# Decode step of a hybrid NSA and latent-attention layer: compressed values from probabilities applied to cached tokens, and cache pages laid eight (latents four) tokens to a partition

## Chip, cores and metric

The kernel is one launch on one core of a Trainium2 chip. All data are fp32. The metric is the device time of the launch in microseconds. The engines named here are TensorE (PE), VectorE (DVE), ScalarE (ACT), GpSimd (POOL) and SyncE (SP); SP issues every DMA of the part of the kernel that is changed.

## What is computed

One decoder layer is applied to a prompt of 1024 tokens and to a decode batch of 8 rows with 4 new tokens each; each row has 2048 cached tokens in 16 pages of 128. Per decode row the reference computes, for the group of 8 NSA heads (2 key-value groups):

```
kc, vc = compress(k_cmp), compress(v_cmp)   # block n: sum over l < 32 of token[16 n + l] @ w[l], plus a constant
p_c    = masked_softmax(q . kc + bias)      # 127 blocks
o_cmp  = p_c @ vc
imp    = p_c @ overlap;  keep the 16 best of 33 blocks of 64 tokens (3 are forced)
o_sel  = softmax over the kept blocks of (q . k_sel + bias) @ v_sel
o_win  = softmax over the last 512 tokens @ v_win
o_a    = gate0 * o_cmp + gate1 * o_sel + gate2 * o_win
```

and for the 4 latent (MLA) heads `o_lat = softmax(q_lat . c + q_rope . k_rope) @ c` over all cached tokens. Then come an output projection and a last RMSNorm. A cached token has 512 numbers in the NSA cache (k_cmp, v_cmp, k_sel, v_sel, each 2 groups of 64) and 192 in the latent cache.

## The kernel before, in words

The launch first does the prompt (projection, preparation, attention, output tiles in `pe_out`), up to about 880 us. Then `pe_decode_loop` and its partners `dve_decode`, `act_decode`, `pool_decode` and `sp_decode` run over the 8 decode rows b = 0 to 7. A row is a fixed sequence written out by hand for each engine; the engines meet by semaphores, and nothing reorders them.

**Loads.** For each row SP reads 16 page numbers (`page_numbers`, L2470), loads 16 pages of the NSA cache (`load_pages`, L2478), the window and the keyed queries (L2489, L2387), and 16 pages of the latent cache (`load_latent`, L2483), then stores the window (L2495). Page n lies in `NSA[b % 2][:, n, :]`, one token to a partition, 2 KB each; latents likewise, 768 bytes each. There are two buffers: the pages of row b + 2 may be issued when `selected_values(b)` has ended (`s_avd`).

**TensorE, one row in order.** `key_products` (L2543) multiplies the turned keys by queries that already hold the key weights, into PSUM banks 3 and 4. `window_scores` (L2565). `compressed_scores` (L2574, L2578) gathers the products into scores on 32 partitions. `latent_scores` (L2592, and L2596 to L2598 for the new tokens) and between its parts `probabilities` (L2612 to L2614), which turns the compressed probabilities. `compress` (L2554): 32 products of 64 rows of turned value tokens by the value weights, for all 127 blocks; inside it the product `fmw` (L2623, which spreads minima over the partitions) and `importance` (L2619). Then `smw` (L2623, sums), `selected_scores` (L2605, into bank 5), `latent_values` (L2631), `window_values`, `compressed_values` (L2648), `fs` (L2623), `ss` (L2623), and at the end `selected_values` (L2653, L2655). In between stand the chunks of the next row (L2339): K0 to K3 turn its compressed keys, V0 to V3 its compressed values, four 128x128 transposes each. Each chunk is copied from PSUM by ACT or DVE into `XT` (L2725, L2730). In the last row a dummy product `keep_warm` (L489) stands ahead of `selected_values`.

**VectorE, one row in order.** Window minima; the compressed scores' minimum; after ACT's exponential the probabilities, also once multiplied by the gate; `selected_turn` (L2819), a transpose of the page keys for the selected scores of the same row; copy of the turned probabilities (L2861); reduction of the latent scores (L2864) and `spread` (L2801), which `fmw` on TensorE waits for; after `fmw` (L2867) the ranking of the blocks (L2871 to L2883); after `smw` scaling and `PTW`; the compressed values' constant (L2893); `PTM` (L2898), the turned latent probabilities that `latent_values` waits for; masking of the selected scores (L2901, L2904), their reduction (L2907) and `spread`, which `fs` waits for; after `ss` scaling and `PTS` (L2920), which `selected_values` waits for; then `window_turn` (L2812) and three `latent_turns` (L2796) of the next row.

**ScalarE.** Copy of the key products, exponentials (L2733), scale of the latent probabilities (L2747), copies of chunks (L2730).

**Order of small products.** Small results and chunks share three PSUM banks in a ring (`RING`); an entry may be written when the one three places earlier has been read.

Of the kernel before, what the change touches and what calls it, by code (L numbers as in the profile page):

```python
# [17 lines left out]
ALU = mybir.AluOpType  # L18
# [96 lines left out]
def build(nc, x_prompt, x_sample, cache_nsa, cache_mla, state_win, page_table, c_prompt, c_sample,  # L115
# [3 lines left out]
    with ExitStack() as ctx:  # L119
# [156 lines left out]
        s_ssq, s_ms, s_rstd, s_xn, s_xt = sem("s_ssq"), sem("s_ms"), sem("s_rstd"), sem("s_xn"), sem("s_xt")  # L276
# [594 lines left out]
        def act_squares(act, j):  # L871
# [3 lines left out]
            if j == 0:  # L875
                act.wait_ge(s_ms, 1)
# [218 lines left out]
        def dve_scale(dve, j):  # L1095

            n = rows(j)
            dve.wait_ge(s_rstd, j + 1)
            dve.tensor_scalar(xs(j)[0:n, :], xs(j)[0:n, :], RSTD[0:n, j:j + 1], None, ALU.mult)\
                .then_inc(s_xn, 1)  # L1100
# [30 lines left out]
        def pool_projection(pool):  # L1131
# [3 lines left out]
            pool.memset(SSQ[:, 0:1], 0.0).then_inc(s_ms, 1)  # L1135
# [58 lines left out]
        def pool_rstd(pool, j):  # L1194
# [4 lines left out]
                .then_inc(s_ms, 1)  # L1199
            pool.wait_ge(s_ms, j + 2)  # L1200
# [831 lines left out]
        def sp_out(sp, tiles, at):  # L2032
            for m, j in enumerate(tiles, at):
# [6 lines left out]
                if m == 2:  # L2040
                    load_queries(sp)
                    load_compressors(sp)
                    load_gates(sp)
# [18 lines left out]
        def pe_out(pe, tiles, at):  # L2062
# [14 lines left out]
            for m, j in enumerate(tiles, at):  # L2077
# [10 lines left out]
                for c in range(2):  # L2088
# [6 lines left out]
                    if m >= 5:  # L2095
                        chunk(pe, 0, ("K0", "K1", "K2", "K3", "V0", "V1")[2 * (m - 5) + c])
# [47 lines left out]
        def act_out(act, tiles, at):  # L2144
            copy = lambda o, i: act.activation(o, i, ACT.Copy)
            for m, j in enumerate(tiles, at):
# [7 lines left out]
                if m >= 5:  # L2154
                    read_chunk(act, copy, 0, ("K0", "K2", "V0")[m - 5])
# [11 lines left out]
        def dve_out(dve, tiles, at):  # L2167
            for m, j in enumerate(tiles, at):
# [25 lines left out]
                if m >= 5:  # L2194
                    read_chunk(dve, dve.tensor_copy, 0, ("K1", "K3", "V1")[m - 5])
# [19 lines left out]
        XT = view(20480, 4096).rearrange("p (k l n) -> p k l n", k=2, l=16)  # L2215
# [8 lines left out]
        VR = dsm(256).rearrange("p (s g e) -> p s g e", s=2, g=G)  # L2224
        PTI, PC, PG = dsm(192), dsm(132), dsm(132)
# [15 lines left out]
        WC2 = view(33152, 4096).rearrange("p (k l m) -> p k l m", k=2, l=16)  # L2241
        QWB = [view(33152 + 512 * n, 512).rearrange("p (l x) -> p l x", l=16) for n in range(2)]
        QSB = view(34176, 256).rearrange("p (b g q) -> p b g q", b=NB, g=G)
# [13 lines left out]
        FM, FI, DQ, HS, LOW = CE[:, 0:128], CE[0:RS, 128:256], CE[:, 256:260], CE[:, 260:262], CE[:, 262:712]  # L2257
# [3 lines left out]
        S_B, W_B, O_B = PS[:, 5, :], PS[:, 6, :], PS[:, 7, :]  # L2261
        W_WIN, W_NEW, W_MLA = W_B[:, 64:192], W_B[:, 192:256], W_B[:, 256:384]
# [5 lines left out]
        CHUNK_ITEMS = [f"K{c}" for c in range(4)], [f"V{c}" for c in range(4)]  # L2268
        SMALL_ITEMS = ["cmp", "pts", "fmw", "imp", "smw", "fs", "ss"]
        KEYED = {(m, c): str(m - 1) for m in range(1, 5) for c in range(2)}  # L2270
        RING = [(0, k + str(n)) for n in range(4) for k in "TAB"]
        RING += [(0, n) for n in CHUNK_ITEMS[0] + CHUNK_ITEMS[1]]
        FRONT = len(RING)
        for b in range(NB):
            more = (lambda *names: [(b + 1, n) for n in names]) if b + 1 < NB else (lambda *names: [])
            RING += [(b, n) for n in SMALL_ITEMS[:5]] + more("K0") + [(b, "fs")] + more("K1", "K2", "K3")
            RING += [(b, "ss")] + more("V0", "V1", "V2", "V3")
# [4 lines left out]
        BY_ACT = {it: it[1] in (("K0", "K2", "K3", "V0", "V2") if it[0] else ("K0", "K2", "V0", "V2", "T0", "T1", "T2", "T3", "B0", "B1", "B2", "B3"))  # L2282
# [10 lines left out]
        DT = ("KWT", "MLT0", "MLT1", "MLT2", "KT", "PTW", "PTM", "PTS")  # L2293

        def turned(b, name):

            return len(DT) * b + DT.index(name) + 1

        def bank_of(b, name):

            m = AT[b, name]
            if m < FRONT:
                if name[0] in "TAB":
                    return PS[:, {"T": 0, "A": 7, "B": 6}[name[0]], :]
                return PS[:, 0 if name == "V3" else 6 + (FRONT - m) % 2, :]
# [11 lines left out]
        def next_bank(pe, b, name):  # L2317

            m = AT[b, name]
            if m < FRONT:  # L2320
                if name in ("K0", "K1"):
                    wait_read(pe, 0, "B3" if name == "K0" else "A3")
                elif name != "V3":
                    wait_read(pe, *RING[m - 2])
            elif (b, name) in SIDE:
                pe.wait_ge(s_cv, 2 * b)
            elif TURN_AT[b, name] == 2:
                wait_read(pe, 0, "V3")
# [4 lines left out]
        def chunk(pe, b, name):  # L2333
            bank = next_bank(pe, b, name)
            k, c = int(name[0] == "V"), int(name[1])
            if name == "K0":
                pe.wait_ge(s_nsa[b % 2], 256 * (b // 2) + 256)
            for n in range(4):
                mm = pe.transpose(bank[:, P * n:P * n + P], NSA[b % 2][:, 4 * c + n, P * k:P * k + P], ident)  # L2339
# [724 lines left out]
```

## Time and profile before

| | us |
|---|---|
| three runs, median (lowest to highest) | 1115.36 (1114.16 to 1116.65) |
| the profiled execution, its own time | 1115.21 |
| span of its instructions | 1113.2 |
| PE busy / DVE busy / ACT busy | 1075.2 / 624.6 / 362.5 |
| mean granted TensorE clock | 0.991 |

The span is the time from the first to the last instruction; the execution's own time is 2.0 us longer. The busy time of an engine counts its work, not its semaphore waits; that of PE is modelled from its issue, so that a high share alone does not say that it limits. The idle time before an instruction, and the engine that ended it, stand in brackets in a timeline.

### The profile page before, as it was taken

What the parts mean: (1) busy time and instruction counts of PE and PEld (TensorE: products, weight loads), DVE (VectorE), ACT (ScalarE), POOL (GpSimd) and SP (SyncE); (2) the same over time, 40 slices, a digit from 0 to 9 for tenths busy, and PEclk for the clock granted to TensorE, in tenths of its full rate; (3) what the DMA queues carried; (4) which work ended last, traced back from release to release, by engine and by line L of the source; (5) the groups of instructions that cost most, each with busy time, mean ns of one, the idle gap of its engine ahead of it and who ended that gap; (6) DMA issues with size and microseconds to landing.
All of it is one profiled execution on the core that took longest, in us unless ns stands there. A gap on an engine that the chain in (4) does not pass through costs nothing. (4 is left out here: it accounts for less than half of the span.)

```text
span 1113.2 us, 22587 instructions
## 1 busy us (share of the span) xinstructions
PE 1075.2 (97%) x8368; PEld 763.3 (69%) x8368; DVE 624.6 (56%) x1627; ACT 362.5 (33%) x893; POOL 86.5 (8%) x184
## 2 busy tenths in 40 slices
PE   6899999999999999998999999999999999999997
PEld 3455599998886677776776657664544576777775
DVE  0645323463423477769677766742323588888883
ACT  0322001121112475546555555631112133333330
POOL 0210100110000011101101010011000200000000
PEclk9899999999999999999999999999999999999998
DMA  9933270001006240000000000005794467878781
GB/s 355 310 115 94 72 211 2 16 19 72 1 1 122 44 116 2 1 1 2 1 2 1 2 1 2 1 1 119 169 307 152 142 217 262 271 274 275 261 251 51
DMA packets 96612, 120.25 MB, mean 108 GB/s; under 512 B 31569, under 2 KB 65380, under 8 KB 95480
## 3 DMA queue, kind: packets, MB, share of 16 engines
q1 hardware_dynamic: 96504, 118.81, 34.4%
q8 instruction: 68, 1.11, 0.4%
q14 instruction: 40, 0.33, 0.1%
HBM read 104.41 MB, written 14.36 MB: 107 GB/s over the span
## 5 line engine op out<-in xcount | busy, mean ns | idle before, releaser
L549 PE MATMUL PS<-AR 128*128 128x256 f32 (+2 forms) x896 | 219.7, 403 | 0.0
L549 PEld LDWEIGHTS PS<-AR 128*128 128x128 f32 x896 | 167.8, 190 | 45.2 <-issue 6.2
L2090 PE MATMUL PS<-AR 128*128 128x512 f32 x256 | 112.3, 592 | 0.0
L1747 PE MATMUL PS<-CA,AR 128*128 128x128 f32 x704 | 111.4, 282 | 0.8 <-ACT AR L1821 0.8
L963 DVE TENSOR_TENSOR AR<-PS,AR 128x256 f32<-128x256 f32 (+2 forms) x80 | 36.2, 452 | 134.4 <-PE PS L549 134.3
L1747 PEld LDWEIGHTS PS<-CA,AR 128*128 128x128 f32 x704 | 77.0, 143 | 44.6 <-issue 31.7
L1821 ACT ACTIVATE AR<-PS 128x512 f32<-128x512 f32 (+1 forms) x108 | 58.2, 546 | 125.1 <-PE PS L1747 124.5
L1725 PE MATMUL PS<-AR 128*128 128x65 f32 (+1 forms) x688 | 89.3, 271 | 0.0
L2090 PEld LDWEIGHTS PS<-AR 128*128 128x128 f32 x256 | 47.5, 190 | 54.0 <-issue 54.0
L1725 PEld LDWEIGHTS PS<-AR 128*128 128x128 f32 x688 | 84.3, 192 | 0.0
L1806 ACT ACTIVATE AR<-PS,SM_ 128x512 f32<-128x512 f32 (+4 forms) x192 | 76.6, 471 | 15.9 <-DVE SM_ L1914 8.8
L1700 PE MATMUL PS<-AR 64*128 64x512 f32 (+3 forms) x384 | 74.1, 491 | 6.6 <-ACT AR L1803 3.9
L1835 DVE COPY AR<-PS 128x512 f32<-128x512 f32 (+1 forms) x100 | 57.3, 586 | 15.5 <-PE PS L1747 15.1
L1803 ACT ACTIVATE AR<-PS,SM_ 128x512 f32<-128x512 f32 (+2 forms) x80 | 51.5, 655 | 15.4 <-DVE SM_ L1914 15.3
L760 ACT ACTIVATE AR<-PS 128x256 f32<-128x256 f32 (+2 forms) x20 | 8.0, 402 | 139.7 <-PE PS L549 98.6
L1876 DVE TENSOR_REDUCE SM_<-PS 128x1 f32<-128x512 f32 (+1 forms) x48 | 29.9, 664 | 41.8 <-PE PS L1696 30.2
L1722 PE MATMUL PS<-AR 128*64 128x128 f32 x656 | 50.0, 282 | 1.2 <-DVE AR L1980 1.2
L2183 DVE TENSOR_TENSOR AR<-PS,AR 128x512 f32<-128x512 f32 x16 | 11.1, 692 | 71.0 <-PE PS L2090 71.0
L541 PE MATMUL PS<-AR 128*64 128x128 f32 x896 | 49.8, 273 | 0.0
L541 PEld LDWEIGHTS PS<-AR 128*64 128x64 f32 x896 | 48.8, 137 | 1.3 <-issue 1.2
L1992 POOL TENSOR_TENSOR AR<-AR 128x256 f32<-128x256 f32 x32 | 23.3, 727 | 326.3 <-DVE AR L1980 325.7
L1700 PEld LDWEIGHTS PS<-AR 64*128 64x128 f32 x384 | 28.9, 185 | 26.3 <-ACT AR L1803 11.9
(364 smaller groups left out, 1622.9 us busy)
## 6 DMA issues: line engine op xcount, KB each, us to landing
AR<-in_cache_nsa SPq DMA_DIRECT2D x128, 256.0 KB, 5.0
AR<-in_cache_mla SPq DMA_DIRECT2D x128, 96.0 KB, 3.7
AR<-in_x_prompt SPq DMA_DIRECT2D x16, 512.0 KB, 4.6
AR<-in_w_ada SPq DMA_DIRECT2D x3, 2048.0 KB, 11.4
AR<-in_w_in SPq DMA_DIRECT2D x6, 1024.0 KB, 8.4
AR<-in_w_ada SPq DMA_DIRECT2D x8, 512.0 KB, 4.3
AR<-in_w_out SPq DMA_DIRECT2D x4, 1024.0 KB, 10.0
AR<-in_w_out SPq DMA_DIRECT2D x2, 2048.0 KB, 17.5
```

The lines of the kernel that those rows point to most:

```text
L541: mm = pe.matmul(bank[64 * h:64 * h + 64, P * r:P * r + P], weights[:, k, h, 64 * r:64 * r + 64], tokens[:, k, :], start=(fresh and r == 0 ...
L549: mm = pe.matmul(bank[:, 0:WIDE[g]], tokens[:, k, :], w, start=(fresh and k == 0), stop=(last and k == 3), skip_group_check=True)
L963: return dve.tensor_tensor(out, src, other, ALU.add)
L1700: mm = pe.matmul(scores(u, gi, o, o + P * n), QT[64 * g:64 * g + 64, r, q], keys[64 * g:64 * g + 64, ks], start=True, stop=True)
L1722: mm = pe.matmul(ob[64 * g:64 * g + 64, P * (r % 2):P * (r % 2) + P], (VS1 if kind == "sel" else VW1)[:, kb, g, 0:64], tile, start=(n == 0 ...
L1725: mm = pe.matmul(out, tile, v, start=(n == 0), stop=(n == nb - 1))
L1747: mm = pe.transpose(PS[:, 4 + c % 2, P * (t - t0):P * (t - t0) + P], tile(u, t), ident)
L1803: act.activation(probs(u, gi, lo, hi), sc, ACT.Exp, bias=NM[:, at, gi:gi + 1], scale=-1.0, accum_out=TOT[og % 4][:, slot:slot + 1]).then_i ...
L1806: act.activation(probs(u, gi, lo, hi), sc, ACT.Exp, bias=NM[:, at, gi:gi + 1], scale=-1.0).then_inc(s_exp, 1)
L1821: evac(act, c, lambda o, i: act.activation(o, i, ACT.Copy), s_evA)
L1835: copy(PTB[:, c % 4, 0:nt, :], PS[:, 4 + c % 2, 0:P * nt].rearrange("p (t q) -> p t q", t=nt)).then_inc(done, 1)
L2090: mm = pe.matmul(PS[0:n, 2 + 2 * (m % 2) + c, :], YTO[m % 2][:, f, 0:n], weights[:, f, 512 * c:512 * c + 512], start=(f == 0), stop=(f == 7))
```

## The change

1. **Compressed values.** `compress`, `compressed_values`, the chunks V0 to V3, their copies and the constant's addition go. The 127 probabilities are spread on four times 32 partitions (`compressed_scores` now issues each product four times, for four groups of 32 columns), ACT multiplies them by the gate into `PX` by four small instructions, `value_turns` turns them (2 transposes), ACT copies them into `PV`, and `value_sums` multiplies them with the cached value tokens as they were loaded (4 products of 512 columns, each on 64 columns of the array). ACT copies the result to `TV`, `value_back` turns it (4 transposes), ACT copies it to `TT_`. The value weights are applied once: `value_products` for rows 0 to 6 in the middle of row 7 and for row 7 before its `selected_values`, in place of `keep_warm`.
2. **Layout.** A page's 128 tokens lie eight to a partition, on 16 partitions that are eight apart (16 KB in a row); latents four to a partition, on 32 partitions. The pages are issued in the order 0, 4, 1, 5, ... of those offsets. The chunk copies become plain 512-column copies.
3. **Order.** `selected_scores` moves from behind `smw` to ahead of `probabilities`, into bank 3. `key_products` and `window_scores` of row b + 1 move ahead of `selected_values(b)`. On DVE `selected_turn` of row b + 1 moves to the end of row b, and `window_turn` ahead of the reading of `fs`. ACT now copies K1 also.
4. **Small loads.** The mask's 4 loads become 16; POOL builds a diagonal of gates ahead of row 0.

```diff
-        XT = view(20480, 4096).rearrange("p (k l n) -> p k l n", k=2, l=16)
+        XT_FLAT = view(20480, 2048)
+        XT = XT_FLAT.rearrange("p (t l c h g) -> p t l c h g", t=2, l=8, c=8, h=2)
...
+S2_B = PS[:, 3, :]
...
             for t in range(TS):
-                sp.dma_start(NCBF[t:RS:TS, 119:127], U_dram[:, 142 - t:142 - t + 113:16],
+                for i in range(4):
+                    sp.dma_start(NCBF[32 * i + t:32 * i + 32:TS, 119:127], U_dram[:, 142 - t:142 - t + 113:16],
...
-            for n in range(lo, hi):
-                sp.dma_start(NSA[b % 2][:, n, :],
-                             cache_nsa[0, bass.ds(pages[n], 1)].rearrange("o t c g d -> (o t) (c g d)")).then_inc(s_nsa[b % 2], 16)
+            for m in range(lo, hi):
+                tile, at = m // 8, 4 * (m % 2) + m % 8 // 2
+                sp.dma_start(NSA[b % 2][at:P:8, 8 * tile:8 * tile + 8, :],
+                             cache_nsa[0, bass.ds(pages[8 * tile + at], 1)].rearrange("o (h l) c g d -> (o h) l (c g d)", l=8))\
+                    .then_inc(s_nsa[b % 2], 16)
...
-                sp.dma_start(MLD[b % 2][:, n, :], cache_mla[0, bass.ds(pages[n], 1)].rearrange("o t c -> (o t) c"))\
+                sp.dma_start(MLD[b % 2][n % 4:P:4, 4 * (n // 4):4 * (n // 4) + 4, :],
+                             cache_mla[0, bass.ds(pages[n], 1)].rearrange("o (h l) c -> (o h) l c", l=4))\
...
+            def value_turns(b):
+                bank = next_bank(pe, b, "pv")
+                pe.wait_ge(s_ex, 6 * b + 2)
+                for t in range(2):
+                    mm = pe.transpose(bank[:, P * t:P * t + P], PX[:, P * t:P * t + P], ident)
+                mm.then_inc(s_it, 1)
+
+            def value_sums(b):
+                wait_read(pe, b, "pv")
+                for t in range(2):
                     for g in range(G):
-                        mm = pe.matmul(PS[:, 3 + g, 0:128], XT[64 * g:64 * g + 64, 1, l, :],
-                                       WC2[64 * g:64 * g + 64, 1, l, :], start=(l == 0), stop=(l == 15))
+                        mm = pe.matmul(PS[64 * g:64 * g + 64, 4, :],
+                                       PV[:, P * t + 64 * g:P * t + 64 * g + 64],
+                                       NSA[b % 2][:, 8 * t:8 * t + 8, P + 64 * g:P + 64 * g + 64],
+                                       start=(t == 0), stop=(t == 1))
+                mm.then_inc(s_r, 1)
+
+            def value_back(b):
+                bank = next_bank(pe, b, "tt")
+                pe.wait_ge(s_rk, 2 * b + 2)
+                for f in range(4):
+                    mm = pe.transpose(bank[:, P * f:P * f + P], TV[:, P * f:P * f + P], ident)
+                mm.then_inc(s_it, 1)
+
+            def value_products(name, lo, hi):
...
+                for x in range(16):
+                    for g in range(G):
+                        at = 64 * g + 16 * (x // 4)
+                        pe.matmul(bank[64 * g:64 * g + 64, 0:16 * (hi - lo)], WV[:, x, :], TT_[:, lo:hi, x % 4, at:at + 16],
+                                  start=(x == 0), stop=False)
...
-            chunk(pe, 0, "V2")
-            chunk(pe, 0, "V3")
+            key_products(0)
+            window_scores(0)
             for b in range(NB):
                 ahead = (lambda name: chunk(pe, b + 1, name)) if b + 1 < NB else (lambda name: None)
-                key_products(b)
-                if b == 0:
-                    wait_read(pe, 0, "V2")
-                window_scores(b)
                 compressed_scores(b)
-                latent_scores(b, 0, 4)
-                if b == 0:
-                    latent_scores(b, 4, 6)
+                latent_scores(b, 0, 6)
+                selected_scores(b)
                 probabilities(b)
-                if b >= 1:
-                    latent_scores(b, 4, 6)
-                compress(b, 0, 5)
                 pe.wait_ge(s_nm, 4 * b + 2)
                 across(b, "fmw", DMN[:, 0:8])
                 importance(b)
-                compress(b, 5, 16)
-                pe.wait_ge(s_ex, 5 * b + 3)
+                value_turns(b)
+                ahead("K0")
+                if b == NB - 1:
+                    value_products("wa", 0, NB - 1)
+                pe.wait_ge(s_ex, 6 * b + 4)
                 across(b, "smw", SUM[:, 2:4])
-                selected_scores(b)
-                ahead("K0")
+                value_sums(b)
                 latent_values(b, 0, NPG)
                 window_values(b)
-                compressed_values(b)
+                value_back(b)
+                ahead("K1")
...
                 pe.wait_ge(s_nm, 4 * b + 4)
                 across(b, "fs", DMN[:, 8:12])
-                for name in ("K1", "K2", "K3"):
+                for name in ("K2", "K3"):
                     ahead(name)
...
                 across(b, "ss", SUM[:, 0:2])
-                for name in ("V0", "V1", "V2"):
-                    ahead(name)
                 if b == NB - 1:
...
-                    keep_warm(pe, 5, (512, 256))
+                    value_products("wb", NB - 1, NB)
+                else:
+                    key_products(b + 1)
+                    window_scores(b + 1)
                 selected_values(b)
-                ahead("V3")
```

ACT's row and the touched parts of DVE's row:

```diff
+                act.wait_ge(s_cv, b + 1)
+                for h in range(4):
+                    rs = slice(RS * h, RS * h + RS)
+                    ins = act.activation(PX[rs, :].rearrange("p (t c x g) -> p t g c x", t=2, c=8, x=2)[:, :, :, :, h % 2],
...
                 wait_read(act, b, "fmw")
                 expo(SMD, PSF[:, S0:S0 + 544], NMX[:, 2:3], SUM[:, 3:4])
                 expo(SWN, SWN, NMX[:, 3:4], SUM[:, 2:3])
+                bank = wait_item(act, b, "pv")
...
+                if b + 1 < NB:
+                    read_chunk(act, copy, b + 1, "K0")
...
                 act.wait_ge(s_nm, 4 * b + 3)
                 act.activation(SMD, SMD, ACT.Identity, bias=0.0, scale=RCD[:, 3:4]).then_inc(s_ex, 1)
+                act.wait_ge(s_r, 2 * b + 2)
...
+                copy(TV, PS[:, 4, :]).then_inc(s_rk, 1)
+                copy(TT_[:, b, :, :], wait_item(act, b, "tt").rearrange("p (f x) -> p f x", f=4)).then_inc(s_rA, 1)
                 if b + 1 < NB:
-                    read_chunk(act, copy, b + 1, "K0")
+                    read_chunk(act, copy, b + 1, "K1")
                 wait_read(act, b, "fs")
                 expo(SSD, SSD, NMX[:, 1:2], SUM[:, 1:2])
                 if b + 1 < NB:
-                    for name in ("K2", "K3", "V0", "V2"):
+                    for name in ("K2", "K3"):
                         read_chunk(act, copy, b + 1, name)
...
-                selected_turn(b)
-                if b == 0:
+                    selected_turn(0)
...
                 bank = wait_item(dve, b, "pts")
...
-                dve.tensor_copy(PTI, bank[:, 0:192]).then_inc(s_rD, 1)
+                dve.tensor_copy(PTI, bank[:, 0:128]).then_inc(s_rD, 1)
...
                 spread(b, 8, 1, MN[:, 2:3])
+                if b + 1 < NB:
+                    window_turn(b + 1)
                 bank = wait_item(dve, b, "fs")
...
                 if b + 1 < NB:
-                    read_chunk(dve, dve.tensor_copy, b + 1, "V1")
-                    window_turn(b + 1)
-                    read_chunk(dve, dve.tensor_copy, b + 1, "V3")
                     latent_turns(b + 1)
+                    selected_turn(b + 1)
```

## Rows read from the trace of the kernel before

**Rows 1.** Timeline of PE, one row: start us, duration us, engine, line, operation
```profile
963.15 0.30 PE L2653 MATMUL PS<-AR 128*32 128x128 f32 x1 [0.46 <-DVE AR L2920]
...
964.36 0.66 PE L2339 MATMUL PS<-CA,AR 128*128 128x128 f32 x4
964.94 1.16 PE L2543 MATMUL PS<-AR 64*32 64x128 f32 x64
...
967.53 0.41 PE L2574 MATMUL PS<-AR 128*32 128x127 f32 x2
...
972.36 0.48 PE L2612 MATMUL PS<-CE,AR 32*128 32x128 f32 x2
...
975.42 1.39 PE L2554 MATMUL PS<-AR 64*128 64x128 f32 x20
976.74 0.39 PE L2623 MATMUL PS<-AR,CE 128*128 128x8 f32 x2
...
980.20 3.68 PE L2605 MATMUL PS<-AR 128*128 128x512 f32 x8
983.71 0.60 PE L2339 MATMUL PS<-CA,AR 128*128 128x128 f32 x4
...
989.62 0.30 PE L2653 MATMUL PS<-AR 128*32 128x128 f32 x1 [0.46 <-DVE AR L2920]
```

**Rows 2.** Groups of PE by line, 860 to 1100 us
```profile
L2554 PE MATMUL PS<-AR 64*128 64x128 f32 x512 | 32.9, 278 | 0.0
```

**Rows 3.** Timeline of DVE, the same row
```profile
965.98 3.47 DVE L2796 STREAM_TRANSPOSE AR<-AR 128x1024 f32<-128x1024 f32 x3
...
972.08 2.29 DVE L2819 STREAM_TRANSPOSE AR<-AR 128x2048 f32<-128x2048 f32 x1
974.31 0.31 DVE L2861 COPY AR<-PS 128x192 f32<-128x192 f32 x1
975.53 0.72 DVE L2864 TENSOR_REDUCE AR<-PS 128x1 f32<-128x544 f32 x1 [0.91 <-PE PS L2598]
...
982.89 0.72 DVE L2898 STREAM_TRANSPOSE AR<-AR 128x544 f32<-128x544 f32 x1
983.91 0.66 DVE L2901 TENSOR_TENSOR AR<-PS,AR 128x480 f32<-128x480 f32 x1 [0.30 <-PE PS L2605]
...
985.52 0.23 DVE L2801 TENSOR_SCALAR AR<-CE,AR 128x4 f32<-128x4 f32 x1
...
990.38 0.68 DVE L2812 STREAM_TRANSPOSE AR<-AR 128x512 f32<-128x512 f32 x1
```

**Rows 4.** Timeline of ACT, the same row
```profile
986.51 0.75 ACT L2733 ACTIVATE AR<-AR 128x544 f32<-128x544 f32 x1 [1.05 <-DVE AR L2910]
```

**Rows 5.** The page's costliest groups: a plain copy of 512 columns from PSUM by ACT
```profile
L1821 ACT ACTIVATE AR<-PS 128x512 f32<-128x512 f32 (+1 forms) x108 | 58.2, 546 | 125.1 <-PE PS L1747 124.5
```

**Rows 6.** Timeline of SP's queue
```profile
870.59 2.88 SPq L2450 DMA_DIRECT2D AR<-rel_by_distance  x4
...
964.68 9.70 SPq L2478 DMA_DIRECT2D AR<-in_cache_nsa  x16
...
991.62 8.21 SPq L2478 DMA_DIRECT2D AR<-in_cache_nsa  x14
```

**Rows 7.** Landing of L2478, 962 to 992 us
```profile
DMA to landing us min/median/max: 2.6/4.7/6.4
```

**Rows 8.** Windows: us, busy of PE, PEld, DVE, ACT, POOL, granted clock, DMA share, GB/s
```profile
973.00:978.00 5.00, 5.00 (x46) 3.75 (x48) 3.27 (x8) 0.64 (x2) 0.00 (x0) 1.00 1.03 367
...
887.00:889.00 2.00, 2.00 (x10) 1.57 (x10) 1.64 (x7) 0.00 (x0) 1.54 (x3) 0.50 1.04 384
...
1094.00:1101.00 7.00, 7.00 (x50) 5.06 (x49) 1.75 (x5) 0.36 (x2) 0.00 (x0) 0.51 0.09 27
```

**Rows 9.** Timeline of PE: ahead of row 0, and the dummy product of row 7
```profile
885.06 2.16 PE L2565 MATMUL PS<-AR 128*128 128x192 f32 x8 [2.73 <-POOL AR L2979]
...
1096.17 2.91 PE L489 MATMUL PS<-CA 128*128 128x512 f32 x4
```

More of the change, by code:

```diff
@@ L2153, in act_out @@
                     key_turns_copy(act, copy, KEYED[m, 0])
[L2154 to L2155 removed]
+                if 5 <= m < 7:
+                    read_chunk(act, copy, 0, ("K0", "K2")[m - 5])
                 act.wait_ge(s_g2, 2 * m + 2)
@@ L2266, in quad @@
             return ap[RS * (n % 4):RS * (n % 4) + RS, 0:128]
-        CHUNK_ITEMS = [f"K{c}" for c in range(4)], [f"V{c}" for c in range(4)]
-        SMALL_ITEMS = ["cmp", "pts", "fmw", "imp", "smw", "fs", "ss"]
+        CHUNK_ITEMS = [f"K{c}" for c in range(4)]
         KEYED = {(m, c): str(m - 1) for m in range(1, 5) for c in range(2)}
         RING = [(0, k + str(n)) for n in range(4) for k in "TAB"]
-        RING += [(0, n) for n in CHUNK_ITEMS[0] + CHUNK_ITEMS[1]]
+        RING += [(0, n) for n in CHUNK_ITEMS]
         FRONT = len(RING)
@@ L2275, in build @@
             more = (lambda *names: [(b + 1, n) for n in names]) if b + 1 < NB else (lambda *names: [])
-            RING += [(b, n) for n in SMALL_ITEMS[:5]] + more("K0") + [(b, "fs")] + more("K1", "K2", "K3")
-            RING += [(b, "ss")] + more("V0", "V1", "V2", "V3")
+            last = (lambda *names: [(b, n) for n in names]) if b + 1 == NB else (lambda *names: [])
+            RING += [(b, n) for n in ("cmp", "pts", "fmw", "imp", "pv")] + more("K0") + last("wa") + [(b, "smw"), (b, "tt")]
+            RING += more("K1") + [(b, "fs")] + more("K2", "K3") + [(b, "ss")] + last("wb")
         SIDE = {(b, n): 3 + k for b in range(1, NB) for k, n in enumerate(("K2", "K3"))}
@@ L2643, in window_values @@
                 pe.matmul(quad(O_B, 0), PTW[:, 4, :], VN[:, 128:256], start=False, stop=False)
-            def compressed_values(b):
-                pe.wait_ge(s_cv, 2 * b + 2)
-                for s in range(2):
-                    pe.matmul(quad(O_B, 1 + s), PTI[:, 128 + 32 * s:160 + 32 * s],
-                              VR[:, s, :, :].rearrange("p g e -> p (g e)"), start=False, stop=False)
             def selected_values(b):
@@ L2733, in expo @@
                 act.activation(out, src, ACT.Exp, bias=bias, scale=-1.0, accum_out=total).then_inc(s_ex, 1)
-            read_chunk(act, copy, 0, "V2")
+            act.wait_ge(s_scr, 256)
+            act.wait_ge(s_gsb, 192)
             for b in range(NB):
```

235 lines of the change are left out of this document (133 added, 102 removed).

## The prediction

> **What bounds the kernel now.** I looked first at the page's busy time, where TensorE stands far ahead of the others, and at its share by stretch, which stays near the whole in the decode rows; so the next view was TensorE's timeline over one row [rows 1]. From the first product of `selected_values` at 963.15 us to the same product one row later at 989.62 is 26.47 us, and nearly every instruction starts where the last one stopped; the one idle bracket is 0.46 us, ended by DVE's `PTS`. So TensorE's own work sets the row. The timelines of DVE [rows 3] and ACT [rows 4] must be read beside it, not because they limit now, but because they form a chain that TensorE's work hides: the minima product `fmw` starts at 976.74, and the transpose L2898 that `latent_values` needs ends at 982.89 + 0.72 = 983.61, 6.9 us later; the `spread` L2801 for `fs` ends at 985.75. Between `fmw` and `latent_values` TensorE has 44 of the 64 `compress` instructions, `selected_scores` and K0. SP works through a row in 991.62 - 964.68 = 26.94 us [rows 6], so it has little air either.
>
> **TensorE's work.** Removed per row: `compress`, 32.9 / 8 = 4.1 us [rows 2]; four value chunks of 0.58 us each (964.36 to 964.94 [rows 1]), 2.3; two small transposes and `compressed_values`, about 0.3. Added: `value_sums`. Eight passes of 512 columns took 983.71 - 980.20 = 3.5 us as `selected_scores` [rows 1]. Two halves of the array can work side by side, as the 64-row pairs of `compress` do: 64 instructions of 128 columns in 4.1 us are 64 ns each, against 3.5 / 8 / 4 = 110 ns for 128 columns of a full product. The bounds are 1.8 us (both halves at once) and 3.5 (one after another); I take 1.8, since both have columns of their own. Six further transposes 0.8; the fourfold score products 0.1 to 3.3 (by the code 10 instructions become 40; at 110 ns each that is 3.3 more; but the four column groups are as independent as the quarters of `selected_values`, 17 products in 964.36 - 963.15 = 1.21 us, so 0.1). Net 6.7 - 2.7 = 4.0 us less, and the 0.46 of idle time goes as well. If TensorE still set the row it would take about 22.3.
>
> **The chain that comes out from under it.** I follow one row of the new order with the durations of now, from `selected_values` to `selected_values`.
>
> *A, on TensorE.* `selected_values` 1.21; compressed scores and four latent products 972.36 - 967.53 = 4.83, plus 0.1; the other two latent products and the new tokens 975.42 - 972.84 = 2.58; `selected_scores` 3.51; `probabilities` 0.25. Sum 12.5. DVE isn't late here: its turns for the row, 3.47 + 2.29 [rows 3], and the minima and probabilities run beside this and end before `probabilities`. By my sum it then sits for about 6 us at the copy of the turned probabilities, since `selected_scores` now stands ahead of them and the latent reduction stands behind that copy on DVE.
>
> *B, nothing for TensorE to do.* The copy L2861 takes 0.31, and from the start of the reduction L2864 (975.53) to `fmw` (976.74) it is 1.21. TensorE waits 1.5 us, because `fmw` is its next instruction.
>
> *C, from `fmw` to the end of `PTM`.* Now 6.9. The constant's addition (0.3) goes, but `PTM` then waits for ACT's scale instead: 6.8. TensorE has `importance`, two transposes, K0, `smw` and `value_sums` here, some 3.5 us; the rest is waiting: about 0.9 for ACT's exponentials and its copy of `PV`, and 2.5 for `PTM`. This is the cover that is gone: `compress` and `selected_scores`, 6 us, used to stand here.
>
> *D, from `PTM` to the next `selected_values`.* Masking, reduction and spread are 985.75 - 983.91 = 1.84, and 0.1 for the second subtraction; `window_turn` 0.68; the reading of `fs` with two hops 0.4; ACT still ends its copy of K1, 0.3; exponential 0.75 [rows 4]; the copies of K2 and K3, 2 x 0.55 [rows 5]; then `key_products` and `window_scores`, 967.53 - 964.94 = 2.59 [rows 1], which cover `ss` and `PTS`. Sum 7.8.
>
> A row is 12.5 + 1.5 + 6.8 + 7.8 = 28.6 us, 2.1 more than 26.47, with TensorE idle for some 6 us of it. The present row added up in the same way, engine by engine with its waits, gives 26.4.
>
> **Other queues.** SP loses nothing in count: 32 page loads, window, store, page numbers. At 26.94 us a row it stays under 28.6. The mask's 12 extra loads, at 2.88 / 4 = 0.72 us each [rows 6], delay row 1's pages by 8.6 us, to about 900 us with their landing; K0 of row 1 comes at about 902 (row 0 of the sum below), so this costs nothing, and up to 2 us if I am wrong by that. POOL's diagonal, two short instructions, stands ahead of the queries that row 0 waits for (2.73 us idle [rows 9]); against this the prompt's end loses two value chunks, 2 x 0.58 us: no change. The pages of row b + 2 are released at the end of `selected_values(b)` and wanted by K0 11.3 + 1.5 + 0.9 = 13.7 us later; K0 can slip 3 us before it delays `latent_values`, so they have 16.7. Now the sixteen issues end 9.7 us after the first began [rows 6] and the last lands some 6 us later [rows 7], 15.7; at 367 GB/s [rows 8] 4.19 MB are 11.4 us. The layout has no row of its own: between 11 (as fast as now, issued earlier) and, if two engines share one path, 23. I take the rate as it is, costing nothing.
>
> **Sum.** The profiled execution took 1115.21 us (span 1113.2), the median run 1115.36: the same within noise. Row 0: ahead of `fmw` 3.5 + 0.25 + 1.5 stand in place of 0.5 and 20 `compress` instructions (1.3), +3.5; behind it C, D and 1.2 give 15.8 where it was 990.83 - 976.74 = 14.1, +1.7: +5. Rows 1 to 6: 6 x 2.1 = +13. Row 7: `wa` is covered by the ranking, mostly; `wb`, 72 small passes, replaces the dummy product of 2.91 us [rows 9] in a stretch where the clock is half [rows 8]: between -1 and +4, I take +1.5. Together +19.5: 1115.2 + 19.5 = 1135.
>
> **Rivals.** *Work sets the row (faster).* If DVE and ACT kept pace, rows would follow TensorE to 22.3, but not below SP's loop, 25 us without back-pressure; 8 rows x (25 - 26.5) and the ends give 1105; it decides only if C's 6.8 us find some 6 us of cover on TensorE. For: TensorE is the bound now and 4 us of it go. Against: the 6.9 us of C are in the trace and have no cover. Chance 0.15. *Half-hidden.* If half of the waits close up the gain and loss cancel, 1113 to 1118: 0.05. *The clock falls in the gaps.* [...] If it falls once per row, the work behind `PTM` (2.6 us up to `fs`) takes up to 2.6 more; part of it is hidden by DVE, I take 1.7: 8 x 1.7 = 13.6, so 1148. Chance 0.2. *The pages come late.* Sixteen partitions, eight apart, one DMA engine each: if engines share a path in pairs, a page takes twice its time, 2 x 11.4 = 23 and 2.6 for the landing [rows 7], 25.4 where 16.7 are free: up to 8.7 us in each of 6 rows, up to 1187; with half of that, 1161. Chance 0.08; it decides from 16.7 us on. [...]
>
> **How the numbers follow.** A run of this kernel can be told from no change by about 0.2%, 2 us. Forecast, 1128 to 1143 by the bounds of the ends and hops: 0.52; the clock case 0.2; late pages 0.08; even 0.05; faster 0.15. The range leaves out the late pages and the larger part of the faster case: 1106 to 1160.
>
> **What would show it.** Right: a row period near 28.6; TensorE idle before the latent value products, ended by DVE's `PTM`, about 2.5 us, and before `fmw` about 1.5; DVE idle some 6 us ahead of the copy of `pts`; K0 not waiting for a DMA. Wrong: rows under 26; a granted clock of 0.5 in each row; K0 or `selected_turn` released by the loading of `in_cache_nsa`.

## The result and the profile after

| | before | changed |
|---|---|---|
| median of 4 runs each, us | 1114.76 (1110.56 to 1116.65) | 1176.51 (1174.56 to 1180.68) |
| ratio, 95% interval | 1 | 1.0564 (1.0522 to 1.0606) |
| span of the profiled execution, us | 1113.2 | 1172.8 |
| granted clock over the span | 0.991 | 0.957 |

The direction was forecast, the size was not: 1176.5 us stand where I had 1135, above the range (1106 to 1160) and inside the rival "the pages come late" (up to 1187, chance 0.08).

The page of the changed kernel: busy time, and the costliest of the decode's groups.

```profile
PE 1062.1 (91%) x8172; PEld 739.4 (63%) x8172; DVE 600.1 (51%) x1588; ACT 368.3 (31%) x958; POOL 87.9 (7%) x186
PEclk8999999999999999999999999999998988888897
L2353 PE MATMUL PS<-CA,AR 128*128 128x128 f32 x128 | 21.5, 308 | 51.5 <-DMA AR<-in_cache_nsa 51.5
```

TensorE's busy time fell by 13 us and the span grew by 60. The third row names nearly all of it: the key chunks (`ahead`, L2353) sat 51.5 us idle for the loading of `in_cache_nsa`. The waits of TensorE in the decode (us in total, times, longest) show where the rest is:

```profile
PE PS L2353 <- DMA AR<-in_cache_nsa: 51.5, 7, 7.9
PE PS L2670 <- DVE AR L2869: 11.4, 8, 1.5
PE PS L2559 <- ACT AR L2768: 5.5, 7, 0.8
...
```

One row of the changed kernel, TensorE's timeline; it answers to [rows 1]:

```profile
1001.51 0.39 PE L2670 MATMUL PS<-AR,CE 128*128 128x8 f32 x2 [1.48 <-DVE AR L2869]
...
1009.70 1.09 PE L2353 MATMUL PS<-CA,AR 128*128 128x128 f32 x4 [7.30 <-DMA AR<-in_cache_nsa]
1010.58 0.43 PE L2670 MATMUL PS<-AR,CE 128*128 128x2 f32 x2
1010.93 3.16 PE L2574 MATMUL PS<-AR 128*64 128x512 f32 x8
1014.03 1.08 PE L2678 MATMUL PS<-AR 128*32 128x128 f32 x32
...
1018.23 0.38 PE L2670 MATMUL PS<-AR,CE 128*128 128x2 f32 x2 [0.41 <-ACT AR L2771]
1019.41 1.15 PE L2559 MATMUL PS<-AR 64*32 64x128 f32 x64 [0.79 <-ACT AR L2768]
1020.48 1.57 PE L2612 MATMUL PS<-AR 128*128 128x192 f32 x8
1021.98 0.30 PE L2696 MATMUL PS<-AR 128*32 128x128 f32 x1
...
1035.55 0.39 PE L2670 MATMUL PS<-AR,CE 128*128 128x8 f32 x2 [1.48 <-DVE AR L2869]
...
1043.94 1.09 PE L2353 MATMUL PS<-CA,AR 128*128 128x128 f32 x4 [7.51 <-DMA AR<-in_cache_nsa]
```

`selected_values` (L2696) starts at 919.24, 953.68, 987.94, 1021.98, 1056.17, 1090.17, 1124.47 and 1155.63: a period of 34.2 us, where 26.47 was [rows 1] and 28.6 was forecast. The wait ahead of `fmw` (L2670, 1.48) is there as forecast, and so is the rest of the chain; the wait ahead of `latent_values` (L2678) is gone, because K0 has already waited 7.30. Between the two `fmw` lines stand 34.04 us.

The loading, in SP's timeline of the row, which answers to [rows 6], and in the windows, which answer to [rows 8] (the last three numbers: granted clock, DMA share, GB/s):

```profile
1023.45 11.19 SPq L2492 DMA_DIRECT2D AR<-in_cache_nsa  x16
...
1035.92 10.34 SPq L2498 DMA_DIRECT2D AR<-in_cache_mla  x16
1046.30 1.09 SPq L2511 DMA_DIRECT2D out<-AR  x2
1057.63 4.62 SPq L2492 DMA_DIRECT2D AR<-in_cache_nsa  x7
```

```profile
1003.00:1010.00 7.00, 0.30 (x2) 0.33 (x3) 3.16 (x7) 0.68 (x4) 0.00 (x0) 0.51 0.93 246
1010.00:1016.00 6.00, 6.00 (x61) 3.45 (x60) 4.08 (x10) 1.94 (x3) 0.00 (x0) 0.71 1.01 385
...
1025.00:1035.00 10.00, 9.07 (x27) 4.24 (x25) 3.57 (x13) 2.52 (x6) 1.07 (x3) 1.00 1.02 241
```

Three things are to be read here. The pages move at 241 to 246 GB/s while the DMA engines are as good as full (0.93 to 1.02); the latents, four tokens to a partition, move at 385. One page's issue costs SP 496 ns (median in the trace) and one of the latents 472, where both cost 333 before; sixteen page loads with all between them take 11.19 us for 9.70. And while TensorE waits for K0's pages its clock falls: over 1003 to 1010 us it is 0.51, and it stays down into the row's next products (0.71 over 1010 to 1016). By the place in the execution, the 59.6 us of span are: the first `selected_values` 9.0 later (919.24 against 910.22); the six periods 46.4 more (205.23 against 158.81); the last one 1.2 (31.16 against 29.97); what follows it 3.0 (17.2 against 14.2).

### The profile page after: what moved, and what is told of

It reads as the page before. It is cut to its first block and busy times, and to the rows that moved or that the text cites. A ratio compares the mean times of both kernels' runs of the same rounds, so it can differ in the third digit from the quotient of the medians.

```text
span 1172.8 us, 22226 instructions
## 1 busy us (share of the span) xinstructions
PE 1062.1 (91%) x8172; PEld 739.4 (63%) x8172; DVE 600.1 (51%) x1588; ACT 368.3 (31%) x958; POOL 87.9 (7%) x186
## 5 line engine op out<-in xcount | busy, mean ns | idle before, releaser
L1747 PE MATMUL PS<-CA,AR 128*128 128x128 f32 x704 | 111.4, 282 | 0.8 <-ACT AR L1821 0.8
L1747 PEld LDWEIGHTS PS<-CA,AR 128*128 128x128 f32 x704 | 76.9, 142 | 44.6 <-issue 31.4
L2353 PE MATMUL PS<-CA,AR 128*128 128x128 f32 x128 | 21.5, 308 | 51.5 <-DMA AR<-in_cache_nsa 51.5
L2768 ACT ACTIVATE AR<-PS 128x512 f32<-128x512 f32 (+3 forms) x62 | 28.6, 500 | 85.8 <-PE PS L2353 50.3
L2353 PEld LDWEIGHTS PS<-CA,AR 128*128 128x128 f32 x128 | 16.9, 162 | 55.1 <-issue 55.1
L1876 DVE TENSOR_REDUCE SM_<-PS 128x1 f32<-128x512 f32 (+1 forms) x48 | 29.9, 664 | 41.8 <-PE PS L1696 30.2
```

The costliest lines, as they stand in the source:

```text
L1747: mm = pe.transpose(PS[:, 4 + c % 2, P * (t - t0):P * (t - t0) + P], tile(u, t), ident)
```

## The experiments

Eleven kernels, each timed in three rounds beside the kernel before, whose medians in these runs lay between 1113.3 and 1115.0 us. The base is the changed kernel, if nothing else is said.

**1. The pages loaded as before** (one token to a partition), the rest as changed:

```diff
-            for m in range(lo, hi):
-                tile, at = m // 8, 4 * (m % 2) + m % 8 // 2
-                sp.dma_start(NSA[b % 2][at:P:8, 8 * tile:8 * tile + 8, :],
...
+            for n in range(lo, hi):
+                sp.dma_start(NSA[b % 2][:, n, :],
```

> The changed kernel with the pages loaded as in the kernel before (one token to a partition, 128 pieces of 2 KB; the latents stay as changed). The tokens then stand in other places than the products suppose, so the values are not the reference's; the work and its order are the changed kernel's. Theory of the late pages: the wait of K0 (7.3 to 7.9 us a row) goes and some 40 us come back; what is left of the loss is the order. Theory of the order (the chain of the prediction): a row of about 28.6 us, 1.5 us of TensorE idle ahead of the minima product, about 2.5 ahead of the latent value products, 1135 us in all, up to 1148 if the clock still falls in each row. Rival: the pages are the whole loss, TensorE's smaller work then sets the row, and the time is at or under the kernel before, 1105 to 1115.

1143.56 us (1137.64 to 1149.79), ratio 1.0275 (1.0228 to 1.0322). TensorE's waits:

```profile
PE PS L2353 <- DMA AR<-in_cache_nsa: 12.9, 6, 3.8
PE PS L2668 <- DVE AR L2867: 11.4, 8, 1.5
...
PE PS L2676 <- DVE AR L2952: 2.2, 4, 1.3
```

33 of the 62 us go with the pages' layout, and the time is inside the range that the order theory gave (1135 to 1148). K0's wait did not go, though, as that theory had it; it fell from 51.5 to 12.9 us. Three of the periods are 28.2 to 28.3 us, the forecast's 28.6, with K0 waiting up to 1.6 us in them; the other three of the first six are 30.0 to 31.8.

**2. What of the layout is slow: the pieces or the partitions?** Three kernels. In the first a page goes to the same sixteen partitions in 2 KB pieces instead of one of 16 KB; in the second to 32 partitions, four apart, in 8 KB; in the third the layout stays and the pages are issued in order instead of in pairs four apart:

```diff
-                             cache_nsa[...].rearrange("o (h l) c g d -> (o h) l (c g d)", l=8))\
+                             cache_nsa[...].rearrange("o (l h) c g d -> (o h) l (c g d)", l=8))\
```

```diff
-                sp.dma_start(NSA[b % 2][at:P:8, 8 * tile:8 * tile + 8, :],
+                sp.dma_start(NSA[b % 2][n % 4:P:4, 4 * (n // 4):4 * (n // 4) + 4, :],
```

```diff
-                tile, at = m // 8, 4 * (m % 2) + m % 8 // 2
+                tile, at = m // 8, m % 8
```

> The changed kernel with the same 16 partitions eight apart to a page, but in pieces of 2 KB (each partition takes every sixteenth token, so eight pieces instead of one of 16 KB; the values are not the reference's). Theory that engines share a path when 16 partitions lie eight apart: no gain; pages still move at 210 to 262 GB/s, a 2 KB packet takes about 135 ns instead of 84, the time stays at 1170 to 1185 us. Rival, that a piece of 16 KB is slow in itself: packets of 84 ns, about 390 GB/s, K0 waits under 1 us, the time falls to that of the first experiment.

> The changed kernel with the pages laid as the latents are, four tokens to a partition, 32 partitions four apart, pieces of 8 KB (values not the reference's). Shared-path theory: full rate, 8 KB packets of about 313 ns and 380 to 400 GB/s, as the latents reach 400 in the changed kernel; K0's wait goes; the rest is set by the order (28.6 us a row) or by SP, whose issues take 0.70 us each in this form against 0.51, a loop of about 29.8 us: 1135 to 1150 us. If the large pieces are slow in themselves: about 500 ns for 8 KB, 250 to 300 GB/s, and over 1150 us.

> The changed kernel with the pages issued in the order of their partitions, 0 to 7, not in pairs four apart. Shared-path theory: four pages in a row then use the same half of the paths, two engines on each: packets of 16 KB take about 1200 ns and the rate stays under 220 GB/s where it reached 262, K0 waits 2 to 4 us longer in a row, 1190 to 1205 us. Rival, that the order is indifferent: 1170 to 1182 us, packets of 1080 ns.

1188.48 us (1186.23 to 1191.54), ratio 1.0652 (1.0611 to 1.0694), for the small pieces; 1154.63 (1151.57 to 1156.91), 1.0362 (1.0325 to 1.04), for four tokens; 1194.89 (1194.2 to 1200.23), 1.0738 (1.0681 to 1.0795), for the pages in order. A window of 10 us while pages are moved, of each of the three in this order (the last three numbers: clock, DMA share, GB/s):

```profile
1037.00:1047.00 10.00, 9.23 (x28) 4.40 (x26) 3.56 (x13) 2.52 (x6) 0.91 (x3) 1.00 1.04 228
```

```profile
1015.00:1025.00 10.00, 7.15 (x27) 3.75 (x25) 3.65 (x13) 4.06 (x12) 1.54 (x3) 0.97 0.96 342
```

```profile
1036.00:1046.00 10.00, 9.52 (x28) 4.46 (x27) 3.57 (x13) 2.52 (x6) 0.61 (x2) 1.00 1.03 223
```

The small pieces came 3 us above their range (1170 to 1185), the pages in order inside theirs, and four tokens to a partition missed by 5 us (1135 to 1150): 22.2 us of K0's wait were left there and not none. In that kernel SP's loop takes 30.4 us, and SP hardly waited for anyone between 900 and 1130 us (0.3 us but for once at either end), so its time doesn't tell what the full rate alone is worth.

The DMA share is nearly the same in all (0.96 to 1.04), so an engine is occupied by its packets in each; only what it moves in that time differs. A 2 KB packet took 152 ns here (median) against 84 with the old loads: the size of the pieces isn't it. With twice the partitions, four apart, an 8 KB packet took 309 ns, 26.5 bytes per ns; a 16 KB packet of the changed kernel took about 1080, 15.2 bytes per ns, which for 16 engines makes 243 GB/s, the rate of the windows (241 to 246). So here it is the set of partitions that a page goes to that sets the rate (241 GB/s for sixteen eight apart, 342 for 32 four apart); whether by their number or by their spacing, these runs don't part. And the order counts: issued one after another, the packets take about 1250 ns, the pages move at 223 GB/s and the kernel is 18 us slower; so the pairs four apart do give something, but not the 342 GB/s of the 32 partitions. What lies behind this was not shown: the shared paths of the expectations are my supposition, no trace shows one. The kernel with four tokens to a partition leaves the pages' turn on DVE as it is, so only its time counts; a complete version of it wasn't tried.

**3. The new pages in the kernel before**, nothing else changed:

```diff
-                sp.dma_start(NSA[b % 2][:, n, :],
...
+                sp.dma_start(NSA[b % 2][at:P:8, 8 * tile:8 * tile + 8, :],
```

> The kernel before with nothing changed but the page loads, which are those of the changed kernel (values not the reference's). Late-page theory: the pages land about 20 us after their release; K0 stands 19.3 us behind it in this order, so it waits only 1 to 2 us, but SP's loop with issues of 0.70 us is about 27 to 28 us a row against 26.5: 1120 to 1135 us. Rival, that the loss of the change lies in the layout alone: the row comes near 34 us and the time near 1170.

1138.13 us (1136.92 to 1140.95), ratio 1.0213 (1.0174 to 1.0252). TensorE's waits have one new row:

```profile
PE PS L2339 <- DMA AR<-in_cache_nsa: 16.7, 6, 4.0
```

SP's timeline there:

```profile
1003.91 11.70 SPq L2479 DMA_DIRECT2D AR<-in_cache_nsa  x16
...
1034.93 11.46 SPq L2479 DMA_DIRECT2D AR<-in_cache_nsa  x16
```

So the layout alone costs 23 us where it meets the old order (3 us more than the upper end of what was expected), and 33 where it meets the new one (1176.5 - 1143.6): the new order wants K0 earlier. The 23 us are not the pages' rate alone. A turn of SP's loop is 1034.93 - 1003.91 = 31.0 us, which is also the average period here, and SP waited for TensorE's release in three rows only, 2.4 us in all; so the dearer issues have a part in them, and this run doesn't part the two.

**4. All loads as before**, so that order and products stand alone:

> The changed kernel with pages and latents both loaded as in the kernel before (values not the reference's), so that order and products alone are left of the change. Order theory: K0 no longer waits for more than 1 us in a row, rows are 28.2 to 28.6 us as in the undisturbed rows of the first experiment, and the time is 1130 to 1137 us. Rival, that the earlier place of K0 needs pages sooner than any layout gives them: K0 still waits 2 us or more in every other row and the time stays at 1143.

1141.79 us (1139.01 to 1146.18), ratio 1.026 (1.0207 to 1.0313), within the spread of the first experiment: the latents' layout costs nothing. This is above the range of the order theory (1130 to 1137) and near the rival's 1143, and K0 does wait more than 1 us in each row but the first. Its spans' difference, 1137.2 - 1113.2 = 24.0, is 5.5 up to the first `selected_values`, 16.0 in the six periods, -0.1 in the last and 2.6 behind it. A row with the quick loads:

```profile
982.82 3.68 PE L2651 MATMUL PS<-AR 128*128 128x512 f32 x8
986.34 0.38 PE L2658 MATMUL PS<-CE,AR 128*128 128x128 f32 x2
988.21 0.39 PE L2667 MATMUL PS<-AR,CE 128*128 128x8 f32 x2 [1.48 <-DVE AR L2866]
...
990.34 0.63 PE L2353 MATMUL PS<-CA,AR 128*128 128x128 f32 x4 [1.25 <-DMA AR<-in_cache_nsa]
...
991.02 3.51 PE L2571 MATMUL PS<-AR 128*64 128x512 f32 x8
995.02 1.08 PE L2675 MATMUL PS<-AR 128*32 128x128 f32 x32 [0.50 <-DVE AR L2951]
...
1002.98 0.30 PE L2693 MATMUL PS<-AR 128*32 128x128 f32 x1
```

`fmw` to `latent_values` is 995.02 - 988.21 = 6.81, my 6.8; from there to `selected_values` 7.96, my 7.8. But K0 waits for its pages even here, 1.25 in this row and 2.2 at most: it was placed too early for the loads of before as well. And the eight passes of `value_sums` (L2571) take 3.51, with a granted clock of 0.57 over 991 to 995 us; at 1.00 they take 1.94, below.

**5. The cover put back.** `selected_scores` behind `value_turns` instead of ahead of `probabilities`, with the loads of before; K0 behind `value_back` in the changed kernel; both moves with the loads of before; both moves in the changed kernel:

```diff
-                selected_scores(b)
                 probabilities(b)
...
                 value_turns(b)
+                selected_scores(b)
```

```diff
                 value_turns(b)
-                ahead("K0")
...
                 value_back(b)
+                ahead("K0")
                 ahead("K1")
```

> As the run before, with selected_scores moved from ahead of probabilities to behind the turns of the value probabilities. Order theory: the 3.6 us product then stands in the wait for PTM, DVE's copy and reduction start 3.5 us sooner, a row is about 25.8 us by the chain; the pages, wanted 2 us later than in the run before counted from the minima product but in a shorter row, and SP's loop of 26 to 27 us hold it there: 1112 to 1122 us. Rival, that the products themselves and the falls of the clock cost the time: no more than 3 us less than the run before.

> The changed kernel whole, with its own layout, and with the chunk K0 of the next row moved from ahead of the sums' product to behind value_back, ahead of K1. Late-page theory: the pages are wanted some 8 us later, K0's wait of 7.5 us shrinks to under 2 and SP's loop, 29.8 us, sets the row: 1140 to 1152 us. Rival, that the pages' transfer itself fills the row: K0 waits on and the time stays over 1165.

> The changed kernel with all loads as before, selected_scores behind the turns of the value probabilities and K0 behind value_back (values not the reference's): the new products in the best order I have, with free layout. Order theory: K0 no longer waits for pages, a row is the chain's 25.9 us or SP's loop of 26 to 27, row 0 and row 7 stay 6 and 1 us longer: 1112 to 1122 us. Rival, that the clock and the many short waits hold rows at 27 or more: over 1125.

> The changed kernel whole, with its own layout, K0 behind value_back and selected_scores behind the turns of the value probabilities. If SP's loop with its costlier issues (11.2 and 10.3 us for 16) sets the row, as I think it does once K0 is late, nothing is gained on the run with K0 alone moved: rows of 30.1 to 30.5 us, 1146 to 1151 us. If the chain set the row there: 3 us a row less, 1125 to 1132.

| kernel | loads | us | ratio |
|---|---|---|---|
| scores behind | before | 1135.36 (1132.34 to 1139.18) | 1.0185 (1.0128 to 1.0242) |
| K0 behind | changed | 1150.57 (1149.4 to 1151.96) | 1.0323 (1.0272 to 1.0374) |
| both behind | before | 1126.75 (1122.68 to 1129.87) | 1.0119 (1.0083 to 1.0155) |
| both behind | changed | 1156.53 (1153.5 to 1163.09) | 1.0378 (1.0348 to 1.0408) |

Of the expectations only that for K0 behind held (1140 to 1152). The scores behind brought 6.4 us, more than the rival's 3 and much less than the 20 of the order theory (1112 to 1122): K0's wait for its pages grew to 15.8 us in seven rows, 3.1 at most, and the periods are 27.0 to 31.3. Both behind is 5 us above its range with the loads of before (1112 to 1122) and 6 above it with the changed ones (1146 to 1151).

Both moves with the old loads, one row on TensorE:

```profile
997.36 0.30 PE L2693 MATMUL PS<-AR 128*32 128x128 f32 x1
...
1007.29 0.39 PE L2667 MATMUL PS<-AR,CE 128*128 128x8 f32 x2 [1.28 <-DVE AR L2865]
...
1008.01 3.60 PE L2651 MATMUL PS<-AR 128*128 128x512 f32 x8
...
1011.65 1.94 PE L2571 MATMUL PS<-AR 128*64 128x512 f32 x8
1014.87 1.08 PE L2675 MATMUL PS<-AR 128*32 128x128 f32 x32 [1.27 <-DVE AR L2950]
...
1023.30 0.30 PE L2693 MATMUL PS<-AR 128*32 128x128 f32 x1
```

Its six periods are (1075.85 - 917.44) / 6 = 26.4 us, those of the kernel before [rows 1], with 3.7 us of waits in the row shown (1.28, 1.27, 0.32 and 0.79); its two shortest periods, 25.94 and 25.95, are the 25.9 that the chain was expected to take. What TensorE saves per row is then eaten by waits, and no more than that. The 13 us that remain of its ratio are not in the rows: the first `selected_values` is at 917.44 against 910.22, the last period is 31.1 against 30.0, and from the last one to the end it is 17.2 us against 14.2. With the changed loads the same two moves don't get there, as TensorE's and DVE's waits show, first for K0 behind:

```profile
PE PS L2678 <- DVE AR L2953: 14.8, 7, 2.7
...
PE PS L2670 <- ACT AR L2771: 10.8, 14, 1.1
```

```profile
DVE AR L2879 <- DMA AR<-sample_q_by_key_weights: 17.7, 7, 3.5
```

and for both:

```profile
DVE AR L2879 <- DMA AR<-sample_q_by_key_weights: 31.9, 7, 7.3
```

With K0 behind alone, K0 no longer waits for its pages (L2353 has no row among the waits), but `window_turn` (L2879) now waits for the window and the keyed queries, which are issued behind the pages on SP's queue; its semaphore counts both, and the queries, issued last, are the releaser named. With both moves K0 waits again (L2353, 13.0 us in six rows, 3.9 at most). SP is the bound: from its timeline, K0 behind,

```profile
983.63 11.16 SPq L2492 DMA_DIRECT2D AR<-in_cache_nsa  x16
...
1006.45 1.10 SPq L2511 DMA_DIRECT2D out<-AR  x2
1013.91 11.14 SPq L2492 DMA_DIRECT2D AR<-in_cache_nsa  x16
```

a turn of SP's loop is 1013.91 - 983.63 = 30.3 us, the period of the rows (30.7 on average), and SP waited for nobody between 900 and 1130 us save once at either end. Quicker products then only lengthen the waits for loads, DVE's from 17.7 to 31.9 us and TensorE's from nothing to 13.0, which is why both moves together gave nothing over one. (The profiled execution with both moves was the longest of its four, 1163.09 us, so its waits are on the high side.)

**6. Does the lost clock cost anything?** To the kernel with all loads as before, products whose result nobody reads, so that TensorE is busy ahead of `fmw`, of K0 and of `latent_values`:

```diff
+            def warm(times):
+                for _ in range(times):
+                    pe.matmul(PS[:, 7, 384:512], ident, CA[:, 0:128], start=True, stop=True)
...
                 probabilities(b)
+                warm(5)
...
                 value_turns(b)
+                warm(4)
                 ahead("K0")
...
                 value_sums(b)
+                warm(4)
```

> The run with all loads as before (1142 us) with dummy products of 128 columns in TensorE's waits: 5 ahead of the wait for the minima product, 4 ahead of K0's pages, 4 ahead of the latent value products, none longer than its wait. [...]

I expected 4 to 12 us less if the falls of the clock cost time, and under 3 less if they come where TensorE waits anyway. 1140.47 us (1137.45 to 1141.99), ratio 1.0247 (1.0224 to 1.027), against 1141.79. The clock over the span is 0.987 in place of 0.975, and it stays at the full level in most of the rows, as the page's strip of forty slices shows (the decode is its last nine). The exceptions are the end, and the first whole row, where K0 waits 2.21 us and the products behind it run at the half clock (0.63 granted over 932 to 936.5 us); a later row has them at full clock (1.00 over 1019 to 1022 us):

```profile
PEclk8999999999999999999999999999999999999997
```

```profile
932.14 1.09 PE L2353 MATMUL PS<-CA,AR 128*128 128x128 f32 x4 [2.21 <-DMA AR<-in_cache_nsa]
...
933.38 2.87 PE L2571 MATMUL PS<-AR 128*64 128x512 f32 x8
...
1018.98 0.63 PE L2353 MATMUL PS<-CA,AR 128*128 128x128 f32 x4 [1.58 <-DMA AR<-in_cache_nsa]
...
1019.65 1.94 PE L2571 MATMUL PS<-AR 128*64 128x512 f32 x8
```

`value_sums` is back at 1.94 us, 1.6 less than at half clock, yet the period is 28.8 on average against 29.1, and the whole time is the same within what these runs can tell. Row by row the two traces say more. In the five periods where the clock held (1.00 granted over 945 to 1087 us), the average is (1087.45 - 945.22) / 5 = 28.4 us against (1090.49 - 944.57) / 5 = 29.2 without the dummies. Two that were 28.3 with `value_sums` at half clock are 28.5 and 28.4 now: there the fall was free, the 1.6 us go into the dummies and the wait for `PTM`, which DVE ends either way. The three others, 30.1, 29.8 and 29.4, are now 28.3 to 28.5. In two of these K0 also waits less (0.6 and 1.6 us for 2.2 and 2.1), so not all of it need be the clock's; in the third K0 waits as long (1.8 for 1.5), and the 0.9 us are the clock's. So the falls are paid in part inside the waits, and not wholly. Against the 3.7 us of these five periods stand the first period, 30.6 for 28.9, and the last, 31.1 for 29.9; in the last row K0 has no pages to wait for, so that eight of the dummies in front of `latent_values` and eight more are work added: from `fmw` to `latent_values` it is 8.6 us there against 7.1. This is one profiled execution of each kernel, and a placement without the surplus dummies wasn't tried.

## Why the prediction was wrong

**The chain from part A to part D** was right. The shortest periods with the loads of before are 28.2 to 28.3 us where I had 28.6; A and B together 13.6 (974.64 to 988.21) for 14.0, C 6.81 for 6.8, D 7.96 for 7.8. The wait ahead of `fmw` is 1.48 for 1.5, DVE's idle time ahead of the copy of `pts` 5.8 for 6, and `value_sums` 1.94 for 1.8, against 3.60 for eight full passes, so the two halves of the array do run side by side. The fourfold score products came at about 1.4 us, against 1.2 for the single ones. The wait for `PTM`, 2.5 by the forecast, was at most 1.3 with K0's wait, and `value_sums` at half clock, ahead of it, and absent in the rows with the longest waits; with K0 moved away it was 2.1 on average and 2.7 at most.

**The failed step: "The layout has no row of its own: between 11 (as fast as now, issued earlier) and, if two engines share one path, 23. I take the rate as it is, costing nothing."** The pages moved at 241 GB/s, not 367. From the first issue to K0's start it is 1043.94 - 1023.45 = 20.5 us where I had 15.7 and the bound was 25.4. K0 arrived at 1043.94 - 7.51 = 1036.4, 13.0 after the issue, for which I had 13.7. The wait of 51.5 us over seven rows, 7.4 in each, is the rival's, in its place and within its price ("up to 8.7"); it lengthened the row by 34.2 - 28.3 = 5.9. No run shows a path that engines share in pairs: the factor of two in the 23 and the 25.4 was my supposition. What the runs showed in its place is a rate that goes by the partitions and the order: 223 GB/s in order, 241 in pairs, 342 with 32 partitions four apart. At 241 the 4.19 MB take 17.4 us, between the 11.4 of the forecast and the 23 of the supposition; pairing gave 18 us of time, and not the 367 of [rows 8]. I had the supposition, its consequence and its price, and gave it 0.08; neither end of the bound had a row of the trace under it, and the point estimate took the cheap one. Half the distance, 4 us in a row, would have put the forecast near 1160.

**The slack** of "3 us" behind K0 was smaller. By it the loads of before should have cost nothing: 15.7 for 16.7. The landing was as I had it (waits of 1.3 to 2.2 us for 15.7 - 13.7), but with the wait the clock falls and `value_sums` takes 3.5 us, 1.6 more. Two rows with waits of 1.25 and 1.48 bear that at 28.3; one with 1.52, in which the clock was down already for K0 itself (1.09 us for its four products in place of 0.63), took 29.4, and three with 2.1 to 2.2 took 28.9, 29.8 and 30.1. With the clock held by dummy products, waits of 1.5 to 1.8 gave 28.5.

**SP "stays under 28.6"** was wrong. I took the number of its issues, which hardly changed, and not what each costs: 496 ns for the pages and 472 for the latents in place of 333 (the traces' medians), 32 times in a row, so SP's loop came to 30.3 us and was the bound once K0 was out of the way (K0 behind).

**The ends.** With the loads of before row 0 came 5.5 us later for my 5 (9.0 in the changed kernel, where K0 waits 6.3 us in row 0 too), the last period cost nothing, and the tail 2.6; I had 1.5 for the last two. Six rows x 2.1 were 13; measured 16.0 with the quick loads, the 3 being K0's wait and the clock behind it.

**The clock rival** (0.2, 13.6 us): the clock did fall in every row, as that rival had it (0.85 granted over each of the six periods), from K0's wait more than from `PTM`'s (0.94 over 1014 to 1045 us with K0 behind, where only the shorter waits are left). Its price, 1.7 us in each of 8 rows (half the clock, 0.50 as in [rows 8], over 2.6 us of work, part of it hidden), was too high: with the quick loads holding the clock gave 0.7 us a row in five rows of the trace, and 1.3 us in the whole time, where the intervals of both kernels overlap.

**What it adds up to.** Order and products alone +28 us (fourth experiment), the pages' layout +33 to 35 on top, of which 23 come with the old order too, SP's dearer issues among them (third experiment). "Work sets the row" fell: no kernel's average period came under 26.4.

## What to carry to other kernels

Here the price of a change of where a transfer lands came from which partitions it reaches (241 GB/s for sixteen eight apart, 342 for 32 four apart), and not from the size of its pieces (228 in 2 KB ones): if no row of the trace shows the shape, measure it alone, and until then place the forecast between the bounds, not at the end that costs nothing. Count a queue by what one issue of the new shape costs and not only by how many there are. When work is moved out of a stretch, list what it covered: with the same loads the same products gave rows of 29.1 or of 26.4 us on average, according to where two of them stood.

## What was not expected of the hardware

An issue on SP whose target has two levels (every fourth or eighth partition, several pieces) took 472 to 496 ns where the plain one took 333, and 557 with eight pieces of 2 KB to a partition. Sixteen partitions eight apart were filled at 223 to 256 GB/s with the DMA engines busy all the time (share 0.95 to 1.04), whether by 2 KB or 16 KB packets, and 32 partitions four apart at 342 (pages) and 385 (a window of mostly latents). Two products with 64 output rows each, in their own halves of the array, took 1.94 us for eight passes of 512 columns, against 3.60 for eight full ones.
